# Forget bias from three bf16 pieces in one product, and a reordered passage into the sparse pairs, in a two-layer decoder trunk

## The chip, the cores and the metric

The kernel runs on one core of a Trainium2 chip. The metric is the device time of one execution in microseconds (us); lower is better. The engines are called PE (TensorE, matmuls), DVE (VectorE), ACT (ScalarE), POOL (GpSimd) and SP (SyncE, which issues the weight loads).

## What is computed

Two decoder layers over 256 tokens of width 2048, all in float32, one sequence. Layer 0 mixes with native sparse attention (8 heads: compressed, selected and window branches, gated) and multi-head latent attention (8 heads) behind one input projection. Layer 1 mixes with forgetting attention (FoX, 16 heads of 128). Each mixer is followed by a SwiGLU network; shifts, scales and gates come from a condition vector through `ada_w`. What the change touches, cut from the reference:

```python
# layer 0: compressed keys and values from blocks of 32 tokens, stride 16, plus a position term
blk = k[:, idx] + pos_emb[:, None, :]
return jax.nn.silu(blk @ w1) @ w2
# layer 1: forget bias of head h: cumulative log forget gates
cum = lax.cumsum(jax.nn.log_sigmoid((f + f_b).astype(jnp.float32)), axis=1).transpose(0, 2, 1)
logit = (jnp.einsum('bqhd,bkhd->bhqk', qq, k) * scale + cq[..., None] - cum[:, :, None, :])
p = masked_softmax(logit, kpos[None, :] <= t[:, None])
```

The residual is `x + g1 * y` with `g1` a row of 2048 gates, made from `ada_w` (accumulated in ACC, summed over partitions by PE) and a bias row in GROW.

## The kernel before

Every weight matrix is streamed in units of 1 MB through a ring of four slots (RAW). ACT rounds a unit to its high part (WHI, line 662), DVE subtracts for the low part (WLO, line 1858), and PE multiplies three times: high by high, low by high, high by low (lines 1129 to 1131). WHI and WLO hold two units each, taken in turn by the unit's number. Between the weight units stand "ada" units: DVE adds a 128-row slab of `ada_w`, times the condition, into ACC (line 1871). SP issues the loads in one fixed order; each waits until its slot of the ring is released, by a low part, an ada step or, for the compression weights, by PE.

The order of work on each engine is written out by hand, with semaphores between the engines; nothing is scheduled by a planner.

**The passage into the sparse pairs.** The input projection is eight chunks; chunk 5 and 6 are the latents of the second branch, chunk 7 (88 columns, line 1147) the gates and the rotary key. On PE follow: turning chunk 6 (L1195), the scores of pair 0 (L1431), the gate row's sum over partitions in four quarters (`finish((0, G1))`, L1176; quarters 2 and 3 reuse the banks of 0 and 1 and wait until DVE has read them), the turn of the gate tile (L1471), and then the loop over 8 pairs of heads. In iteration p stand a unit of the compression product (`cmp_unit`, L1411: 16 products of 30 stationary columns), scores p+1, values p-1 (L1460 to L1463) and the turn of pair p's probabilities (L1442). Pairs 0 to 3 are the selected branch, 4 to 7 the window branch. DVE does in this stretch: RMS scaling of chunk 6 (ST, L2104), its gain (TF, L2125), the low part CQL (L1965), the copy of the gate tile (GK, L2099), logits of pair 0 (L2159 to L2164), the four additions into GROW (L1882), gates (L2196, L2197), the blocks BF (L2206, eight additions), then per iteration logits, an ada step, outputs of the pair before. ACT does in each iteration the exponentials (L838) and the copy of the turned probabilities PT (L848); in iteration 7 the high part of the first MLA weight stands between the two.

BF lies in the room of AHI/ALO, the split input of the projection, so the blocks can be written only after the last projection product. GK shares the buffer TF with the latents, so it waits for CQL.

**FoX scores.** Eight pairs of heads (12 to 19), one batch (`fox_scores`) within each of eight chunks of the projection, after the chunk's first unit. For each head and each block of 128 queries a batch has three products into one bank: query by key (L1740), the bias (L1741: stationary a column of the identity broadcast to 128 columns over 16 rows, moving CUMT, the 16 heads' cumulative sums by token, f32), and the mask (L1742, bf16). CUMT is made once, during the chunk before: cumulative sums (CUM, L2605), turned on PE (L1777), scaled by DVE (L2608).

Of the kernel before, what the change touches and what calls it, by code (L numbers as in the profile page):

```python
# [23 lines left out]
KT = D // P  # L24
# [17 lines left out]
C_ID, C_UT, C_ONE, C_NEG, C_THR, C_INV, C_CM, C_CN = 0, 128, 256, 384, 512, 513, 545, 575  # L42
C_BLK, C_LEAD = 605, 609
C_ALL = 610

# [145 lines left out]
class Machine:  # L191

    def __init__(self, nc, t, ctx, known):
# [19 lines left out]
        self.WHI = sb("WHI", [P, 2, 2048], F32R)  # L213
        self.WLO = sb("WLO", [P, 2, 2048], F32R)

        ((self.AHI, self.ALO), (_, self.XG), (self.O, self.KN, self.RP, self.KRO, self.HCT, self.KCT, self.VCN), (_, self.BF)) = overlay(
            [("AHI", [P, KT, T], F32R), ("ALO", [P, KT, T], F32R)],
            [("XG_ROOM", [P, KT, T], F32), ("XG", [P, KT, T], F32)],
            [("O", [P, 16, T], F32), ("KN", [P, 8, T], F32), ("RP", [P, 2, 8, 64], F32), ("KRO", [P, 2, P], F32),
             ("HCT", [P, 2, 2, 30], F32), ("KCT", [P, 32], F32), ("VCN", [P, 2, P], F32)],  # L220
            [("O_ROOM", [P, 16, T], F32), ("BF", [P, 2, 32, 30], F32)])

# [21 lines left out]
        self.IDB = sb("IDB", [P, P], BF16)  # L244
        self.NEGB = sb("NEGB", [P, P], BF16)
        self.VC = sb("VC", [P, V_ALL])
        self.COND = sb("COND", [P, KT])
# [9 lines left out]
            [("KRR", [P, 2, 64], F32), ("COS", [P, 2, 32], F32), ("SIN", [P, 2, 32], F32)],  # L257
            [("Z", [P, 4, 2, 16], F32), ("CUM", [P, 2, 16], F32)])
        self.PF = sb("PF", [P, 2])
# [13 lines left out]
        self.PART = self.RS[:, 2, 4:6]  # L273
        self.CUMT, self.FZ, self.FE, self.FL = (self.TF[0:16, i, :] for i in range(4))
        self.GK = self.TF[0:88, 0, :]
        self.RB, self.RBS, self.GB, self.FB = (self.VC[:, a:b] for a, b in ((V_RB, V_RBS), (V_RBS, V_GB), (V_GB, V_FB), (V_FB, V_ALL)))
# [834 lines left out]
def tensor_program(block, nc, t, out, m):  # L1111

    @block.tensor
    def _(pe):
# [50 lines left out]

        def finish(v, blocks=range(KT)):

            pe.wait_ge(m["ada_used"].sem, ADA_DONE[v])
            acc = m.adder(v)
            if v[1] in (G1, G2):  # L1170
                if v == (1, G1):
                    wait("t_read", ("fox", m.fox_at["k", 3]))
                for q in range(4):
# [293 lines left out]
        scores(0)  # L1467
        finish((0, G1))
        wait("gk_kept", ("even_in", 7))
        for tb in range(2):  # L1470
            ins = turn(m.PS[:, 4, P * tb:P * tb + 88], m.GK[:, P * tb:P * tb + P], m.CON[0:88, C_ID:C_ID + 88])  # L1471
        m["gk_turned"].tick(ins, 0)
        wait("cmp_b", 0)
        for p in range(8):
            if p == 4:
                wait("cmp_b", 1)
            cmp_unit(p)
            if p == 0:
                wait("gates_in", ("even_in", 7))
                wait("row_read", ((0, G1), 3))  # L1480
            if p < 7:
                scores(p + 1)
            if p:
                values(p - 1)
            turn_p(p)
        values(7)
# [243 lines left out]
        def fox_scores(p):  # L1730
# [4 lines left out]
            for j in range(2):  # L1735
                h = m.pairs[p][1] + j
                bank = m.PS[:, 4 + j, :]
                for tb in range(2):
                    qs, n, at = slice(P * tb, P * tb + P), P + P * tb, P * tb
                    mm(bank[:, at:at + n], m.QT_F[:, h, qs], m.KT_F[:, h, 0:n], start=True, stop=False)  # L1740
                    mm(bank[:, at:at + n], m.CON[0:16, C_ID + h:C_ID + h + 1].to_broadcast([16, P]), m.CUMT[:, 0:n], start=False, stop=False)  # L1741
                    ins = mm(bank[:, at + n - P:at + n], m.IDB[:], m.NEGB[:], start=False, stop=True)  # L1742
# [30 lines left out]
        def cumulate_turned():  # L1773

            wait("cum_ready", 0)
            for tb in range(2):
                ins = turn(m.PS[0:16, 5, P * tb:P * tb + P], m.CUM[:, tb, :], m.ID)  # L1777
            m["cumt_done"].tick(ins, 0)
# [53 lines left out]
def vector_program(block, nc, t, out, m):  # L1832

    @block.vector
    def _(dve):
# [36 lines left out]

        def finish(v):

            layer, seg = v
            n = 2 * layer + (seg >= SH2)
            if seg in (G1, G2):
                wait("grow_bias", 2 * layer + (seg == G2))
                for q in range(4):
                    wait("ada_sum", (v, q))  # L1880
# [214 lines left out]
        def even_first(c):  # L2095
            if c.i == 7:
                chunk_done(c)
                dve.wait_ge(m["lo_split"].sem, m["lo_split"].value)
                m["gk_kept"].tick(V.tensor_copy(m.GK, m.acc(c.buf)[0:88, 0, 0:T]), c.key)  # L2099
# [6 lines left out]
        def bias_masked():  # L2106
            dve.wait_ge(m["bias_kept"].sem, m["bias_kept"].value)
            after = m.CON[:, C_NEG:C_NEG + P].unsqueeze(1).to_broadcast([P, 8, P])
            for at in (0, T):
                ins = TT(m.BIAS[:, :, at:at + P], m.BIAS[:, :, at:at + P], after, ALU.add)  # L2110
            link(ins)

        def even_second(c):
# [8 lines left out]
            else:  # L2122
# [3 lines left out]
                dve.wait_ge(m["tf_ready"].sem, m["tf_ready"].value)  # L2126
                split_lo(c.key, m.CQL[:, at:at + 4, :], m.TF[:], m.CQH[:, at:at + 4, :])

        def even_between(c, j):
# [4 lines left out]
            if c.i == 4 and j == 2:  # L2134
                angles()
        run(m.even_in[3:], even_first, even_second, between=even_between)


        def logits(p):
# [13 lines left out]
            elif name == "fox":  # L2153
                for j in range(2):
                    for tb in range(2):
                        cols = slice(P, 3 * P) if tb else slice(0, P)
                        ins = TS(dst[:, j, cols], m.PS[:, 4 + j, cols], FOX_SCALE, m.CUM[:, tb, h0 + j:h0 + j + 1], ALU.mult, ALU.add)
            else:
# [7 lines left out]
        def outputs(p):  # L2166
# [19 lines left out]
            else:  # L2186
# [11 lines left out]
        for i in range(2):  # L2198
            at = (V_PK, V_PV)[i]
            for g in range(2):  # L2200

                for half in range(2):
                    l0 = 16 * half
                    src = m.XT[:, 8 + 2 * i + g, l0:l0 + 240].rearrange("p (n l) -> p l n", l=16)
                    pos = m.VC[:, at + l0:at + l0 + 16].unsqueeze(2).to_broadcast([P, 16, 15])
                    ins = TT(m.BF[:, i, l0:l0 + 16, 15 * g:15 * g + 15], src, pos, ALU.add)  # L2206
                    m["cmp_b"].tick(ins, i)
        for p in range(8):
# [381 lines left out]
        def fox_between(c, j):  # L2590
# [11 lines left out]
            if c is fox_chunks[0] and j == 3:  # L2602
                fox_second(m.fox_in[1])
                wait("cum_done", 0)
                m["cum_ready"].tick(V.tensor_copy(m.CUM[:], m.PS[:, 4, 0:32].rearrange("p (b h) -> p b h", b=2)), 0)  # L2605
# [70 lines left out]
```

## Time and profile before

| | us |
|---|---|
| median of 3 runs | 2571.3 (2568.48 to 2573.88) |
| the profiled execution | 2571.42 |
| its span, first to last instruction | 2569.6 |
| PE busy | 2480.1 (97%) |
| DVE busy | 1708.0 (66%) |
| ACT busy | 1028.9 (40%) |
| mean granted TensorE clock | 0.985 |

Busy time is the union of an engine's instructions. A matmul's end is modelled, and matmuls overlap; how long one really keeps the engine is best read from the start of the next. The clock is a share of full speed, 1.00 being 2.4 GHz and 0.50 being 1.2 GHz.

### The profile page before, as it was taken

The numbers are of one execution on the slowest core, as the hardware profiler recorded it, in microseconds if no ns is written. First come the engines' busy times: TensorE is split into PE (matmuls) and PEld (weight loads), VectorE is DVE, ScalarE is ACT, GpSimd is POOL, SyncE is SP. The second block draws the span as 40 slices with busy tenths as digits, with TensorE's granted clock in tenths as the row PEclk, the third lists the DMA queues.
The fourth block names the chain that finished last, engine by engine and source line by source line (L and its number), as shares of the span: only waits on it lengthen the run. The fifth ranks groups of instructions, "written<-read, shape, count | busy, mean of one in ns | idle before, by whom it ended". The sixth has DMA issues, their size and how long they took to land.

```text
span 2569.6 us, 29279 instructions
## 1 busy us (share of the span) xinstructions
PE 2480.1 (97%) x11756; PEld 2011.1 (78%) x11756; DVE 1708.0 (66%) x1355; ACT 1028.9 (40%) x975; POOL 3.0 (0%) x9
## 2 busy tenths in 40 slices
PE   5899899999999999999999999999999999999998
PEld 3677577778878888888877888778788788888887
DVE  6878686886676767766766666668766554445446
ACT  2234344454333333343544444444543333333434
POOL 0000000000000000000000000000000000000000
PEclk8899999999999999999999999999999999999999
DMA  9989575868786877778788896889687655555553
GB/s 356 351 292 344 206 277 215 299 242 289 277 311 220 311 269 290 269 265 307 228 182 228 182 211 184 231 264 331 220 288 278 235 190 187 195 181 196 188 189 130
DMA packets 266196, 636.57 MB, mean 248 GB/s; under 512 B 15984, under 2 KB 26992, under 8 KB 244720
## 3 DMA queue, kind: packets, MB, share of 16 engines
q1 hardware_dynamic: 264800, 627.35, 73.7%
q0 software_dynamic: 720, 5.24, 0.6%
q10 hardware_dynamic: 576, 2.57, 0.2%
q8 instruction: 71, 1.16, 0.2%
q14 instruction: 29, 0.24, 0.0%
HBM read 633.03 MB, written 2.10 MB: 247 GB/s over the span
## 4 chain that ended last, share of the span: by engine, by line
PE 82%; DVE 8%; DMA 5%; ACT 3%; issue 2%; SPq 0%; DVEq 0%; ACTq 0%
PE PS L1129 23%; PE PS L1131 23%; PE PS L1130 23%; DVE WLO L1858 2%; ACT WHI L662 2%; DMA RAW<-in_fox_w_in 2%; DMA RAW<-in_even_w_in 1%; PE PS L1411 1%; DVE ACC L1871 1%; DMA PRO<-in_ada_w 1%; DVE ACC L1980 1%; PE PS L1431 1%; PE PS L1180 1%; PE PS L1697 1%; PE PS L1195 1%
## 5 line engine op out<-in xcount | busy, mean ns | idle before, releaser
L1129 PE MATMUL PS<-WHI,AHI 128*128 128x512 f32 x2024 | 796.3, 393 | 11.5 <-DVE WLO L1858 9.8
L1131 PE MATMUL PS<-WHI,ALO 128*128 128x512 f32 x2024 | 788.9, 390 | 0.0
L1130 PE MATMUL PS<-WLO,AHI 128*128 128x512 f32 x2024 | 788.4, 390 | 0.0
L1858 DVE TENSOR_TENSOR WLO<-RAW,WHI 128x2048 fp32r<-128x2048 f32 (+2 forms) x217 | 492.2, 2268 | 350.5 <-ACT WHI L662 350.2
L662 ACT ACTIVATE WHI<-RAW 128x2048 fp32r<-128x2048 f32 (+2 forms) x217 | 412.0, 1899 | 717.6 <-PE PS L1131 509.8
L2448 DVE TENSOR_TENSOR WLO<-RAW,WHI 128x2048 fp32r<-128x2048 f32 x174 | 398.8, 2292 | 351.6 <-ACT WHI L972 351.6
L972 ACT ACTIVATE WHI<-RAW 128x2048 fp32r<-128x2048 f32 x174 | 333.7, 1918 | 578.1 <-PE PS L1131 555.4
L1129 PEld LDWEIGHTS PS<-WHI,AHI 128*128 128x128 f32 x2024 | 380.4, 188 | 94.5 <-issue 7.1
L1131 PEld LDWEIGHTS PS<-WHI,ALO 128*128 128x128 f32 x2024 | 380.3, 188 | 80.3
L1130 PEld LDWEIGHTS PS<-WLO,AHI 128*128 128x128 f32 x2024 | 380.6, 188 | 76.7 <-issue 0.2
L1129 PE MATMUL PS<-WHI,GHI 128*128 128x512 f32 x864 | 340.9, 395 | 3.4 <-DVE WLO L1858 3.1
L1131 PE MATMUL PS<-WHI,GLO 128*128 128x512 f32 x864 | 337.0, 390 | 0.0
L1130 PE MATMUL PS<-WLO,GHI 128*128 128x512 f32 x864 | 336.7, 390 | 0.0
L1871 DVE SCALAR_TENSOR_TENSOR ACC<-RAW,COND,ACC 128x2048 f32<-128x2048 f32 x94 | 220.4, 2345 | 0.7
L1129 PEld LDWEIGHTS PS<-WHI,GHI 128*128 128x128 f32 x864 | 162.6, 188 | 40.2 <-issue 5.3
L1131 PEld LDWEIGHTS PS<-WHI,GLO 128*128 128x128 f32 x864 | 162.4, 188 | 34.2
L1130 PEld LDWEIGHTS PS<-WLO,GHI 128*128 128x128 f32 x864 | 162.7, 188 | 33.3 <-issue 0.5
L2459 DVE SCALAR_TENSOR_TENSOR ACC<-RAW,COND,ACC 128x2048 f32<-128x2048 f32 x60 | 140.7, 2345 | 0.1
L838 ACT ACTIVATE L<-L,NM 128x128 f32<-128x128 f32 x80 | 35.4, 446 | 62.4 <-DVE NM L2164 62.4
L1980 DVE SCALAR_TENSOR_TENSOR ACC<-PRO,COND,ACC 128x512 f32<-128x512 f32 x60 | 45.0, 750 | 6.9 <-DMA PRO<-in_ada_w 5.2
L1286 PE MATMUL PS<-WHI,AHI 128*128 128x512 f32 x96 | 41.5, 432 | 7.0 <-DVE ALO L1965 6.8
L2339 DVE TENSOR_TENSOR TF<-PS,GROW 128x1024 f32<-128x1024 f32 x28 | 34.2, 1221 | 14.7 <-PE PS L1131 14.7
(326 smaller groups left out, 1785.7 us busy)
## 6 DMA issues: line engine op xcount, KB each, us to landing
RAW<-in_ffn_w SPq DMA_DIRECT2D x264, 1024.0 KB, 5.2
RAW<-in_ada_w SPq DMA_DIRECT2D x176, 1024.0 KB, 5.9
RAW<-in_fox_w_in SPq DMA_DIRECT2D x64, 1024.0 KB, 8.2
RAW<-in_even_w_in SPq DMA_DIRECT2D x28, 1024.0 KB, 7.5
PRO<-in_ada_w SPq DMA_DIRECT2D x16, 1024.0 KB, 12.5
RAW<-in_even_w_out SPq DMA_DIRECT2D x16, 1024.0 KB, 7.3
RAW<-in_fox_w_out SPq DMA_DIRECT2D x16, 1024.0 KB, 6.7
GROW<-in_ada_b POOLq DMA_DIRECT2D x4, 1024.0 KB, 6.7
```

Source lines behind the costliest of these rows:

```text
L662: A(m.w_view(m.WHI, u), m.w_view(m.RAW, u), ACT.Copy).then_inc(m["hi_ready"].sem, 1)
L838: m["exp_done"].tick(A(m.L[:, b, h, cols], m.L[:, b, h, cols], ACT.Exp, bias=m.NM[:, b, j:j + 1], accum_out=m.SM[:, b, j:j + 1]), p)
L972: A(m.WHI[:, (up.w0 + j) % 2, :], m.RAW[:, (up.s0 + s) % RING, :], ACT.Copy).then_inc(m["hi_ready"].sem, 1)
L1129: mm(dst(tb), xh, whi[:, k, :], start=first and k == 0, stop=False)
L1130: mm(dst(tb), xh, wlo[:, k, :], start=False, stop=False)
L1131: ins = mm(dst(tb), xl, whi[:, k, :], start=False, stop=last and k == nk - 1)
L1286: mm(dst, xh, whi[:, k, :], start=kt == 0, stop=False)
L1858: TT(m.w_view(m.WLO, u), m.w_view(m.RAW, u), m.w_view(m.WHI, u).bitcast(F32), ALU.subtract).then_inc(m["lo_ready"].sem, 1)
L1871: STT(out=acc[:], in0=raw, scalar=m.COND[:, kt:kt + 1], in1=acc[:], op0=ALU.mult, op1=ALU.add).then_inc(m["ada_used"].sem, 1)
L1980: ins = STT(out=acc, in0=src, scalar=by, in1=acc, op0=ALU.mult, op1=ALU.add)
L2448: TT(m.WLO[:, (up.w0 + j) % 2, :], m.RAW[:, (up.s0 + s) % RING, :], m.WHI[:, (up.w0 + j) % 2, :].bitcast(F32), ALU.subtract).then_inc(m["l ...
L2459: STT(out=m.ACC[:], in0=m.RAW[:, slot, :], scalar=m.COND[:, col], in1=m.ACC[:], op0=ALU.mult, op1=ALU.add).then_inc(m["ada_used"].sem, 1)
```

## The change

Two things, independent of each other.

**Bias.** The cumulative sums are copied six times side by side (96 columns), so that turning them gives 96 rows. DVE scales them and makes three bf16 pieces: the rounded value in rows 0 to 31, the rounded rest in rows 32 to 63, the rounded rest of that in rows 64 to 95. A stationary matrix HEADB (bf16, a one in rows h, 32+h and 64+h of column h) picks head h and adds the three pieces in one bf16 product of 96 rows.

**Passage.** BF moves into half 1 of the WLO ring, the gate tile copy GK into PT. On DVE the blocks and the gate copy come before the gain of chunk 6, two of the four gate-row additions before the first logits, CQL behind them, the other two additions after the gates. On PE compression unit 0 comes between quarters 0, 1 and quarters 2, 3 of the gate row, and in the loop unit p+1 stands ahead of the turn of pair p (before: unit p ahead of scores p+1). DVE waits for the last compression unit before it writes the first MLA low part, since that takes BF's place.

```diff
+        (self.WLO,), (_, self.BF) = overlay(
+            [("WLO", [P, 2, 2048], F32R)],
+            [("BF_ROOM", [P, 2048], F32), ("BF", [P, 2, 32, 30], F32)])
...
-            [("O_ROOM", [P, 16, T], F32), ("BF", [P, 2, 32, 30], F32)])
-            [("Z", [P, 4, 2, 16], F32), ("CUM", [P, 2, 16], F32)])
+            [("Z", [P, 4, 2, 16], F32), ("CUM", [P, 2, 6, 16], F32)])
+        self.CUMB = self.TF[0:96, 0, 0:128].bitcast(BF16)
+        self.CUMV, self.CUMR = self.TF[0:96, 2, :], self.TF[0:96, 3, :]
-        self.GK = self.TF[0:88, 0, :]
+        self.GK = self.PT[0:88, 1, 0, 0:T]
 # tensor engine, passage
         scores(0)
-        finish((0, G1))
+        finish((0, G1), quarters=(0, 1))
         wait("gk_kept", ("even_in", 7))
+        wait("tf_ready", ("even_in", 6))
...
         wait("cmp_b", 0)
+        cmp_unit(0)
+        finish((0, G1), quarters=(2, 3))
+        wait("gates_in", ("even_in", 7))
         for p in range(8):
-            if p == 4:
-                wait("cmp_b", 1)
-            cmp_unit(p)
-            if p == 0:
-                wait("gates_in", ("even_in", 7))
-                wait("row_read", ((0, G1), 3))
             if p < 7:
                 scores(p + 1)
             if p:
                 values(p - 1)
+            if p == 3:
+                wait("cmp_b", 1)
+            if p < 7:
+                cmp_unit(p + 1)
+            if p == 0:
+                wait("row_read", ((0, G1), 3))
             turn_p(p)
 # tensor engine, FoX scores
-                    mm(bank[:, at:at + n], m.CON[0:16, C_ID + h:C_ID + h + 1].to_broadcast([16, P]), m.CUMT[:, 0:n], start=False, stop=False)
+                    mm(bank[:, at:at + n], m.HEADB[0:96, h:h + 1].to_broadcast([96, P]), m.CUMB[:, 0:n], start=False, stop=False)
 # vector engine, passage
         def even_between(c, j):
+            if c.i == 7:
+                blocks()
+                even_first(c)
...
+        finish((0, G1), (0, 1))
         logits(0)
-        finish((0, G1))
+        latent_low(m.even_in[6])
         wait("gk_turned", 0)
...
+        finish((0, G1), (2, 3))
         for p in range(8):
...
+        dve.wait_ge(m["row_used"].sem, m.cmp_in[1][-1].n + 1)
         lo(mla[0])
 # vector engine, FoX
-                m["cumt_ready"].tick(TS(m.CUMT, m.PS[0:16, 5, 0:256], -1.0 / FOX_SCALE, None, ALU.mult), 0)
+                link(TS(m.CUMV, m.PS[0:96, 5, 0:256], -1.0 / FOX_SCALE, None, ALU.mult))
+                link(V.tensor_copy(m.CUMB, m.CUMV))
+                link(TT(m.CUMR, m.CUMV, m.CUMB, ALU.subtract))
+                V.tensor_copy(m.CUMB[32:64], m.CUMR[32:64])
+                link(V.tensor_copy(m.CUMB[64:96], m.CUMR[64:96]))
+                link(TT(m.CUMR[64:96], m.CUMR[64:96], m.CUMB[64:96], ALU.subtract))
+                m["cumt_ready"].tick(V.tensor_copy(m.CUMB[64:96], m.CUMR[64:96]), 0)
```

`blocks()` holds the eight additions that stood ahead of the loop, and `latent_low` the subtraction that makes CQL.

## Rows read from the trace of the kernel before

**Rows 1.** The page, part 1: engine, busy us, share of the span, instructions.

```profile
PE 2480.1 (97%) x11756; PEld 2011.1 (78%) x11756; DVE 1708.0 (66%) x1355; ACT 1028.9 (40%) x975; POOL 3.0 (0%) x9
```

**Rows 2.** Timeline, PE, passage: start us, busy us, line, out<-in, count, idle before.

```profile
266.44 1.88 PE L1176 MATMUL PS<-ACC,CON 128*128 128x512 f32 x4
273.05 3.78 PE L1176 MATMUL PS<-ACC,CON 128*128 128x512 f32 x4 [4.73 <-DVE GROW L1882]
276.62 0.50 PE L1471 MATMUL PS<-CON,TF 88*128 88x88 f32 x2
279.90 5.33 PE L1411 MATMUL PS<-RAW,BF 128*30 128x256 f32 x16 [2.78 <-DVE BF L2206]
285.15 1.58 PE L1431 MATMUL PS<-XT 128*128 128x128 f32 x8
...
287.32 3.64 PE L1411 MATMUL PS<-RAW,BF 128*30 128x256 f32 x16
```

**Rows 3.** Windows: stretch, length, busy of PE, PEld, DVE, ACT, POOL, PEclk, DMA.

```profile
280.00:286.00 6.00, 6.00 (x21) 2.84 (x22) 2.92 (x5) 1.45 (x7) 0.00 (x0) 0.72 0.00 0
286.00:300.00 14.00, 14.00 (x83) 9.52 (x82) 10.36 (x18) 5.35 (x18) 0.00 (x0) 1.00 0.89 308
```

**Rows 4.** Timeline, DVE, the same passage.

```profile
265.33 1.66 DVE L2125 TENSOR_SCALAR TF<-PS,VC 128x256 f32<-128x256 f32 x4 [3.97 <-PE PS L1195]
268.53 1.23 DVE L1965 TENSOR_TENSOR CQL<-TF,CQH 128x1024 fp32r<-128x1024 f32 x1 [1.54 <-ACT CQH L673]
...
270.20 0.94 DVE L2159 SCALAR_TENSOR_TENSOR L<-PS,BIAS 128x768 f32<-128x768 f32 x1
...
272.30 1.29 DVE L1882 TENSOR_TENSOR GROW<-PS,GROW 128x512 f32<-128x512 f32 x2
...
277.91 3.81 DVE L2206 TENSOR_TENSOR BF<-XT,VC 128x240 f32<-128x240 f32 x8
```

**Rows 5.** Windows, a stretch of the FoX stage.

```profile
1400.00:1500.00 100.00, 100.00 (x478) 80.40 (x477) 63.28 (x71) 46.58 (x55) 0.00 (x0) 1.00 0.88 200
```

**Rows 6.** Timeline, all engines, end of the pair loop.

```profile
329.84 0.81 ACT L848 ACTIVATE PT<-PS 128x768 f32<-128x768 f32 x1 [2.50 <-PE PS L1442]
...
332.53 0.40 ACT L838 ACTIVATE L<-L,NM 128x128 f32<-128x128 f32 x1 [1.88 <-DVE NM L2164]
...
334.30 1.47 ACT L662 ACTIVATE WHI<-RAW 128x1536 fp32r<-128x1536 f32 x1
...
335.68 0.78 ACT L848 ACTIVATE PT<-PS 128x768 f32<-128x768 f32 x1
...
336.51 0.49 PE L1460 MATMUL PS<-NV,PT 128*128 128x128 f32 x2 [0.95 <-ACT PT L848]
```

**Rows 7.** Timeline, PE, first FoX score batch; the other seven repeat it.

```profile
1382.77 0.38 PE L1740 MATMUL PS<-KT_F,QT_F 128*128 128x128 f32 x2
1383.08 0.48 PE L1741 MATMUL PS<-TF,CON 16*128 16x128 f32 x2
1383.49 0.23 PE L1742 MATMUL PS<-NEGB,IDB 128*128 128x128 bf16 x1
1383.56 0.65 PE L1740 MATMUL PS<-KT_F,QT_F 128*128 128x256 f32 x2
1384.14 0.69 PE L1741 MATMUL PS<-TF,CON 16*128 16x256 f32 x2
1384.77 0.23 PE L1742 MATMUL PS<-NEGB,IDB 128*128 128x128 bf16 x1
...
1386.93 0.48 PE L1129 MATMUL PS<-WHI,AHI 128*128 128x512 f32 x1
```

**Rows 8.** Timeline, PE, bf16 products of the position bias.

```profile
96.28 1.36 PE L1320 MATMUL PS<-GROW,S 128*128 128x32 bf16 x48
```

**Rows 9.** Timeline, PE, one product pair of the MLA scores.

```profile
407.02 0.70 PE L1433 MATMUL PS<-QRK 64*128 64x256 f32 x2
```

**Rows 10.** Timeline, DVE, the scaling that makes CUMT.

```profile
1377.38 0.41 DVE L2608 TENSOR_SCALAR TF<-PS 16x256 f32<-16x256 f32 x1 [0.32 <-PE PS L1777]
```

More of the change, by code:

```diff
@@ L42 @@
 C_ID, C_UT, C_ONE, C_NEG, C_THR, C_INV, C_CM, C_CN = 0, 128, 256, 384, 512, 513, 545, 575
-C_BLK, C_LEAD = 605, 609
-C_ALL = 610
+C_BLK, C_LEAD, C_STACK = 605, 609, 610
+C_ALL = 642
 V_C, V_MIX, V_FFN, V_QN, V_KVN, V_FQ, V_FK, V_PK = 0, 16, 48, 80, 84, 88, 89, 90
@@ L67, in constants @@
     c[:, C_LEAD] = i % 32 == 0
+    c[:, C_STACK:C_STACK + 32] = i[:, None] % 32 == np.arange(32)[None, :]
     return c
@@ L213, in __init__ @@
         self.WHI = sb("WHI", [P, 2, 2048], F32R)
-        self.WLO = sb("WLO", [P, 2, 2048], F32R)
-        ((self.AHI, self.ALO), (_, self.XG), (self.O, self.KN, self.RP, self.KRO, self.HCT, self.KCT, self.VCN), (_, self.BF)) = overlay(
+        (self.WLO,), (_, self.BF) = overlay(
+            [("WLO", [P, 2, 2048], F32R)],
+            [("BF_ROOM", [P, 2048], F32), ("BF", [P, 2, 32, 30], F32)])
+        ((self.AHI, self.ALO), (_, self.XG), (self.O, self.KN, self.RP, self.KRO, self.HCT, self.KCT, self.VCN)) = overlay(
             [("AHI", [P, KT, T], F32R), ("ALO", [P, KT, T], F32R)],
@@ L219, in __init__ @@
             [("O", [P, 16, T], F32), ("KN", [P, 8, T], F32), ("RP", [P, 2, 8, 64], F32), ("KRO", [P, 2, P], F32),
-             ("HCT", [P, 2, 2, 30], F32), ("KCT", [P, 32], F32), ("VCN", [P, 2, P], F32)],
-            [("O_ROOM", [P, 16, T], F32), ("BF", [P, 2, 32, 30], F32)])
+             ("HCT", [P, 2, 2, 30], F32), ("KCT", [P, 32], F32), ("VCN", [P, 2, P], F32)])
         (self.GHI, self.GLO), (self.PRO,), (self.XT, self.CQH, self.CQL), (_, self.QN), (self.KT_F, self.V_F) = overlay(
@@ L245, in __init__ @@
         self.NEGB = sb("NEGB", [P, P], BF16)
+        self.HEADB = sb("HEADB", [P, 16], BF16)
         self.VC = sb("VC", [P, V_ALL])
@@ L273, in __init__ @@
         self.PART = self.RS[:, 2, 4:6]
-        self.CUMT, self.FZ, self.FE, self.FL = (self.TF[0:16, i, :] for i in range(4))
-        self.GK = self.TF[0:88, 0, :]
+        self.FZ, self.FE, self.FL = (self.TF[0:16, i, :] for i in range(1, 4))
+        self.CUMB = self.TF[0:96, 0, 0:128].bitcast(BF16)
+        self.CUMV, self.CUMR = self.TF[0:96, 2, :], self.TF[0:96, 3, :]
+        self.GK = self.PT[0:88, 1, 0, 0:T]
         self.RB, self.RBS, self.GB, self.FB = (self.VC[:, a:b] for a, b in ((V_RB, V_RBS), (V_RBS, V_GB), (V_GB, V_FB), (V_FB, V_ALL)))
@@ L1164, in unit, with finish @@
             ins.then_inc(m["w_used"].sem, 1)
-        def finish(v, blocks=range(KT)):
+        def finish(v, blocks=range(KT), quarters=range(4)):
             pe.wait_ge(m["ada_used"].sem, ADA_DONE[v])
@@ L1172, in finish @@
                     wait("t_read", ("fox", m.fox_at["k", 3]))
-                for q in range(4):
+                for q in quarters:
                     if q >= 2:
@@ L1776, in cumulate_turned @@
             for tb in range(2):
-                ins = turn(m.PS[0:16, 5, P * tb:P * tb + P], m.CUM[:, tb, :], m.ID)
+                ins = turn(m.PS[0:96, 5, P * tb:P * tb + P], m.CUM[:, tb].rearrange("p r h -> p (r h)"), m.ID)
             m["cumt_done"].tick(ins, 0)
@@ L1871, in ada, with finish @@
                 STT(out=acc[:], in0=raw, scalar=m.COND[:, kt:kt + 1], in1=acc[:], op0=ALU.mult, op1=ALU.add).then_inc(m["ada_used"].sem, 1)
-        def finish(v):
+        def finish(v, quarters=range(4)):
             layer, seg = v
@@ L1878, in finish @@
                 wait("grow_bias", 2 * layer + (seg == G2))
-                for q in range(4):
+                for q in quarters:
                     wait("ada_sum", (v, q))
@@ L1993, in _ @@
         V.tensor_copy(m.IDB[:], m.ID)
+        V.tensor_copy(m.HEADB[:], m.CON[:, C_STACK:C_STACK + 16])
         link(V.tensor_copy(m.NEGB[:], m.CON[:, C_NEG:C_NEG + P]))
@@ L2097, in even_first @@
                 chunk_done(c)
-                dve.wait_ge(m["lo_split"].sem, m["lo_split"].value)
                 m["gk_kept"].tick(V.tensor_copy(m.GK, m.acc(c.buf)[0:88, 0, 0:T]), c.key)
@@ L2111, in bias_masked, with blocks, latent_low @@
             link(ins)
+        def blocks():
+            for i in range(2):
+                at = (V_PK, V_PV)[i]
+                for g in range(2):
+                    for half in range(2):
+                        l0 = 16 * half
+                        src = m.XT[:, 8 + 2 * i + g, l0:l0 + 240].rearrange("p (n l) -> p l n", l=16)
+                        pos = m.VC[:, at + l0:at + l0 + 16].unsqueeze(2).to_broadcast([P, 16, 15])
+                        ins = TT(m.BF[:, i, l0:l0 + 16, 15 * g:15 * g + 15], src, pos, ALU.add)
+                        m["cmp_b"].tick(ins, i)
+        def latent_low(c):
+            at = 4 * (c.i - 5)
+            split_lo(c.key, m.CQL[:, at:at + 4, :], m.TF[:], m.CQH[:, at:at + 4, :])
         def even_second(c):
@@ L2126, in even_second @@
                 dve.wait_ge(m["tf_ready"].sem, m["tf_ready"].value)
-                split_lo(c.key, m.CQL[:, at:at + 4, :], m.TF[:], m.CQH[:, at:at + 4, :])
+                if c.i == 5:
+                    latent_low(c)
         def even_between(c, j):
@@ L2135, in even_between @@
                 angles()
-        run(m.even_in[3:], even_first, even_second, between=even_between)
+            if c.i == 7:
+                blocks()
+                even_first(c)
+        run(m.even_in[3:], even_first, even_second, between=even_between, last=lambda c: None)
         def logits(p):
@@ L2156, in logits @@
                         cols = slice(P, 3 * P) if tb else slice(0, P)
-                        ins = TS(dst[:, j, cols], m.PS[:, 4 + j, cols], FOX_SCALE, m.CUM[:, tb, h0 + j:h0 + j + 1], ALU.mult, ALU.add)
+                        ins = TS(dst[:, j, cols], m.PS[:, 4 + j, cols], FOX_SCALE, m.CUM[:, tb, 0, h0 + j:h0 + j + 1], ALU.mult, ALU.add)
             else:
@@ L2197, in _ @@
         m["gates_in"].tick(TT(m.GATES[:], gk[:, :, 0:24], m.GB[:].unsqueeze(1).to_broadcast([P, 2, 24]), ALU.add), ("even_in", 7))
[L2198 to L2207, printed above, removed]
+        finish((0, G1), (2, 3))
         for p in range(8):
@@ L2604, in fox_between @@
                 wait("cum_done", 0)
-                m["cum_ready"].tick(V.tensor_copy(m.CUM[:], m.PS[:, 4, 0:32].rearrange("p (b h) -> p b h", b=2)), 0)
+                m["cum_ready"].tick(V.tensor_copy(m.CUM[:], m.PS[:, 4, 0:32].rearrange("p (b h) -> p b h", b=2).unsqueeze(2).to_broadcast([P, 2, 6, 16])), 0)
             if c is fox_chunks[1] and j == 0:
                 wait("cumt_done", 0)
-                m["cumt_ready"].tick(TS(m.CUMT, m.PS[0:16, 5, 0:256], -1.0 / FOX_SCALE, None, ALU.mult), 0)
+                link(TS(m.CUMV, m.PS[0:96, 5, 0:256], -1.0 / FOX_SCALE, None, ALU.mult))
[5 more added lines that the diff above has]
+                m["cumt_ready"].tick(V.tensor_copy(m.CUMB[64:96], m.CUMR[64:96]), 0)
             if j == 2 and c.key in m.pair_in:
```

## The prediction

> **What bounds the kernel now.** I read the page's engine table first: TensorE (PE) is busy 2480.1 of 2569.6 us, 97% [rows 1]. So time can only be won where PE idles, where it runs at its lower clock, or by giving it less to do. The change touches two such places.
>
> The first is the passage from the input projection into the sparse pairs. The reader is to see four things in [rows 2]. After the first two quarter products of the gate row (L1176, 266.44 + 1.88 = 268.32) PE waits 4.73 us for VectorE (DVE), which has to add them into GROW. The other two quarters last 3.78 us although the first two took 1.88. Then PE waits 2.78 us for the blocks BF. The first compression unit (L1411) takes 5.33 us, the second 3.64. The granted clock explains the last: 0.72 over 280 to 286 us, 1.00 from 286 [rows 3]; the first unit ran mostly at 1.2 GHz behind the idle time, the second at 2.4. Why DVE is late stands in [rows 4]: latent scaling (TF) to 267.0, its low part to 269.8, first logits from 270.20, only then the two additions (272.30), and the blocks last of all (277.91).
>
> The second place is the forget-bias product in the FoX scores. Over 1400 to 1500 us PE is busy 100.00 of 100.00 us at clock 1.00 [rows 5], so there every matmul taken away counts in full, if nothing else becomes late.
>
> **Part 1, the passage.** DVE's new order puts the blocks and the copy of the gate/rotary-key tile ahead of the latent scaling. BF now lies in half 1 of WLO, whose last unit (odd, of the chunk before) is already consumed, so the blocks can start when DVE has scaled ST, at about 261.35 (an estimate from the trace: it is the end of the work before the 3.97 us idle in [rows 4]: 265.33 - 3.97 = 261.36). They take 3.81 us: 265.2. The copy takes 0.4: 265.6. TF takes 1.66: 267.25, against 266.99 now. All this fills idle DVE time and is ahead of PE.
>
> PE, from 268.32: it no longer waits. The turn of the gate tile takes 0.50 [rows 2] and needs the copy and TF (267.25): 268.8. Compression unit 0 at the full clock 3.6: 272.4. Meanwhile DVE makes additions 0 and 1 as their products end (1.29 for two in [rows 4], so 269.1), then the first logits (272.30 - 270.20 = 2.10: 271.2), the low part (1.23: 272.4), gates (0.5: 272.9). Quarters 2 and 3 on PE: 1.9, 274.3; their additions 275.0, behind PE's scores 1. Scores 1 and turn 0 together 287.32 - 285.15 = 2.17, unit 1 another 3.6: PE has both units and turn 0 done at 280.0. Now it has them done at 287.32 + 3.6 = 290.9. Gain 10.9 us. As a check by another sum: idle 4.73 + 2.78, quarters 3.78 - 1.88 = 1.90, clock 5.33 - 3.64 = 1.69; together 11.1.
>
> What is late next: in the loop each unit now stands ahead of the turn of its pair instead of behind it. For seven iterations that costs nothing, because turn p+1 comes a whole iteration later. At the end it does. Today ScalarE (ACT) empties turn 6 at 329.84, starts the last exponentials at 332.53 and has them done at 334.30, then splits the first MLA weight (1.47), copies PT at 335.68, and PE starts the last values at 336.51 after waiting 0.95 [rows 6]. All this shifts by 10.9, but turn 6 moves another 3.6 later (unit 7 is ahead of it). So ACT copies PT of pair 6 at 322.5 to 323.3, and the exponentials of pair 7, queued behind that copy on ACT, start at 323.3 instead of 332.53 - 10.9 = 321.6. The whole tail behind them (exponentials 1.77, split 1.4, copy 0.8) is 1.7 to 1.8 late: last values at 327.4 instead of 325.6. Part 1 nets **336.5 - 327.4 = 9.1 us**.
>
> The added wait of DVE ahead of the first MLA low part is for unit 7 of the compression, done at 321.7 in this schedule; DVE reaches it at about 326. Behind it are the outputs of pair 7 and all MLA low parts, so it would matter, but it is met 4 us before. SP's queue: loads are released by compression units and ada steps, both earlier, and no load is put past another. The prologue's DVE copy (HEADB) and 32 more constant columns I cost at nothing: the prologue waits for weights. Bounds: not above 10.9 (tail hidden); not below 5.7 (9.1 less 1.7 if the clock does not hold in unit 0, less 1.7 for a second late wait of the size of the tail's).
>
> **Part 2, the bias product.** Each of 8 score batches has two heads with one 128- and one 256-column bias product, f32, two passes. By the starts in [rows 7]: 1383.49 - 1383.08 = 0.41 and 1384.77 - 1384.14 = 0.63, so 2 x (0.41 + 0.63) = 2.08 us of a batch of 1386.93 - 1382.77 = 4.16. New: one bf16 pass with 96 rows. No row has that shape. Nearest: the mask product, bf16, 128 columns, 1383.56 - 1383.49 = 0.07; and 48 bf16 products of 32 columns in 1.36 us, 0.028 each with their weight loads [rows 8]. From 32 to 128 columns that is 0.042/96 a column, so 256 columns come to 0.13. New sum 2 x (0.07 + 0.13) = 0.40; saved 1.68 a batch, times 8 = **13.4 us**. Lower bound: half the old price, one pass for two, saves 1.04 a batch, 8.3. Upper bound: the QK products beside it get cheaper too, down to those of the sparse scores, where four such take at most 1.58 (285.15, [rows 2]); then the batch is 1.58 + 0.40 + 4 x 0.07 = 2.26, saves 1.90, 15.2 in all.
>
> Why the 16-row product is so dear: a 64-row one in the MLA scores is busy 0.70 us for its two passes of 256 columns [rows 9], the 16-row one 0.69 [rows 7], so the price is not the rows but standing between 128-row products. The Trainium skill (TensorE: Matmul & The Clock Gate, Part 2) says that a weight load is pulled ahead of running matmuls when the row groups don't conflict or it goes to the background buffer, and that its time goes by columns, not rows. By the second half alone 96 rows are free; by the first, a 96-row tile among 128-row ones could stay unhidden as the 16-row one does. That is the first rival.
>
> DVE pays for the split: instead of one 0.41 us scaling at 1377.38 [rows 10] seven linked steps on at most 96 x 256, six more of 0.2 to 0.4, some 2.3 us: ready at about 1380, while the scores that wait for it start at 1382.77 [rows 7]. Behind it on DVE is the low part of the next unit, needed after the scores: 1382.2 against 1385.2. Hidden; uncovered it would cost those 2.3 once. Copying CUM sixfold and turning 96 instead of 16 columns are some 0.1 us each. The freed 1.7 us do not make low parts late: DVE is busy 63.28 of 100 [rows 5].
>
> **Sum.** 9.1 + 13.4 = 22.5. The profiled execution took 2571.42 us (span 2569.6), practically the median 2571.3. So 2571.4 - 22.5 = **2549 us**.
>
> **Rivals.**
> A, the weight loads of 96-row products stay unhidden. For: 16- and 64-row products both show it. Against: bf16 loads are short, 0.028 us with their matmul [rows 8]. Price: near the lower bound, 8.3 instead of 13.4: 2571.4 - 17.4 = 2554.
> B, the passage gives more back: ACT's queue (PT copy, exponentials, split) ends the pair loop, and a second such wait follows in the MLA stage. Part 1 at 5.7: 2552. For: PE does wait there now. Against: every load and low part of that stage hangs on events that shift by the same 9.
> C, the neighbours shrink too and the tail is hidden: 10.9 + 15.2: 2545.
> D, the change does not do what it says: PE leaves the quarters but waits for TF or the gate copy. It would need DVE to be 4 us later than reckoned, and ends near 2553.
> E, slower: the low clock, which now ends by itself at 286, persists through the pair loop, since the thin units, turns and row sums come before PE has had a long dense stretch. An iteration costs (336.51 - 279.90) / 8 = 7.1 [rows 2, 6]; by 5.33 against 3.64 about half more at the low clock, 3.5 each. The seventh such iteration takes the last of the 22.5 us gained; all eight cost 28 and give 2577. The Trainium skill's same page (on transposes) says that they don't count as busy the same way for the clock. Against: with just this mix the clock came back at 286 and stayed [rows 3].
>
> **Chances.** Forecast (2546 to 2552) 0.62; A 0.15; B 0.10; C 0.06; D 0.03; E 0.04. The range, 2544 to 2556, takes in both ends of both parts but for E and the corner where all goes badly. No change that can be told is 0.2%, 5.1 us: 2566 to 2576. Faster 0.95, same 0.02, slower 0.03, E's gentler half being the middle case.
>
> **What would show it.** Right: no PE wait for GROW or BF between 268 and 280, granted clock 1.00 there, all L1411 units near 3.6; scores 2 starting near 280; last values near 327.4 after a wait of 0.6 or more behind ACT; score batches of 2.5 us instead of 4.16, with the bias products at 0.07 and 0.13; 1400 to 1500 still 100% busy. Wrong: a 96-row product above 0.2 us, PE waiting for WLO inside the FoX stage, a new wait of DVE on the last compression unit, or a shift of the MLA stage by less than 8 us.

## The result, and the profile after

| | before | after |
|---|---|---|
| median, us | 2569.9 (4 runs, 2567.2 to 2573.9) | 2541.3 (4 runs, 2538.8 to 2543.3) |
| profiled execution, us (span) | 2571.4 (2569.6) | 2538.8 (2536.8) |
| PE busy, us | 2480.1 | 2459.8 |

The ratio is 0.9887, 95% interval 0.987 to 0.9904: 28.6 us or 1.1% faster. 2549 was forecast, 2544 to 2556 the range: the direction was right, and the time lies 7.7 us below the forecast and below the range. The gain itself was put 6.1 us too low (22.5 against 28.6); the other 1.5 us are the starting point, a profiled execution of 2571.4 where the median is 2569.9.

The page of the changed kernel, its span and its engine table (busy us, share, instructions):

```profile
span 2536.8 us, 29223 instructions
...
PE 2459.8 (97%) x11724; PEld 2007.0 (79%) x11724; DVE 1709.1 (67%) x1362; ACT 1027.2 (40%) x975; POOL 3.0 (0%) x9
```

PE's share is again 97% [rows 1]; between the two profiled executions 20.3 us of its work are gone and 12.5 us of its idle time.

The passage on PE, timeline (start, busy us, line, output and inputs, count); it answers to [rows 2]:

```profile
264.67 1.88 PE L1181 MATMUL PS<-ACC,CON 128*128 128x512 f32 x4
266.38 0.32 PE L1477 MATMUL PS<-CON,PT 88*128 88x88 f32 x2
266.63 3.64 PE L1416 MATMUL PS<-RAW,BF 128*30 128x256 f32 x16
270.20 1.98 PE L1181 MATMUL PS<-ACC,CON 128*128 128x512 f32 x4
...
273.42 3.64 PE L1416 MATMUL PS<-RAW,BF 128*30 128x256 f32 x16
...
277.70 1.48 PE L1436 MATMUL PS<-XT 128*128 128x128 f32 x8
```

There is no idle time in it. Quarters 2 and 3 take 1.98 where they took 3.78, unit 0 takes 3.64 where it took 5.33, and scores 2 start at 277.70, 13.03 us behind the first quarter. Before they started at 290.89, 24.45 us behind it, as PE's timeline of the kernel before shows:

```profile
286.57 0.82 PE L1442 MATMUL PS<-CON,L 128*128 128x128 f32 x6
...
290.89 1.58 PE L1431 MATMUL PS<-XT 128*128 128x128 f32 x8
```

DVE in the same stretch, against [rows 4]:

```profile
259.70 3.93 DVE L2131 TENSOR_TENSOR BF<-XT,VC 128x240 f32<-128x240 f32 x8
...
265.82 1.45 DVE L1891 TENSOR_TENSOR GROW<-PS,GROW 128x512 f32<-128x512 f32 x2 [0.29 <-PE PS L1181]
```

The blocks stand at 259.70 in time that DVE spent waiting before, and the first two additions at 265.82, while PE still makes their products. The granted clock (the column behind POOL's busy time) is full over 265 to 280. Before it was 0.50 over quarters 2 and 3 and 0.72 over 280 to 286 [rows 3]; the first line is the kernel before, the second the changed one:

```profile
273.00:277.00 4.00, 3.95 (x6) 1.62 (x6) 1.42 (x3) 0.00 (x0) 0.00 (x0) 0.50 0.00 0
...
265.00:280.00 15.00, 15.00 (x73) 8.75 (x72) 12.73 (x21) 7.83 (x20) 0.00 (x0) 1.00 0.55 167
```

The end of the pair loop, all engines, against [rows 6]:

```profile
320.05 0.81 ACT L853 ACTIVATE PT<-PS 128x768 f32<-128x768 f32 x1 [4.47 <-PE PS L1447]
...
320.92 0.49 PE L1465 MATMUL PS<-NV,PT 128*128 128x128 f32 x2 [0.90 <-ACT PT L853]
...
322.51 1.47 ACT L667 ACTIVATE WHI<-RAW 128x1536 fp32r<-128x1536 f32 x1
...
323.89 0.79 ACT L853 ACTIVATE PT<-PS 128x768 f32<-128x768 f32 x1
...
324.73 0.49 PE L1465 MATMUL PS<-NV,PT 128*128 128x128 f32 x2 [1.19 <-ACT PT L853]
```

Here PE waits for ACT twice, 0.90 for the copy of pair 6 and 1.19 for the copy of pair 7, where it waited once before, 0.95 [rows 6]. That is the price of the new loop order.

The first FoX score batch, against [rows 7]:

```profile
1371.41 0.38 PE L1749 MATMUL PS<-KT_F,QT_F 128*128 128x128 f32 x2
1371.63 0.22 PE L1750 MATMUL PS<-TF,HEADB 96*128 96x128 bf16 x1
1371.69 0.22 PE L1751 MATMUL PS<-NEGB,IDB 128*128 128x128 bf16 x1
1371.75 0.65 PE L1749 MATMUL PS<-KT_F,QT_F 128*128 128x256 f32 x2
1372.23 0.27 PE L1750 MATMUL PS<-TF,HEADB 96*128 96x256 bf16 x1
1372.35 0.22 PE L1751 MATMUL PS<-NEGB,IDB 128*128 128x128 bf16 x1
...
1373.43 0.48 PE L1134 MATMUL PS<-WHI,AHI 128*128 128x512 f32 x1
```

A batch takes 1373.43 - 1371.41 = 2.02 us where it took 4.16 (2.01 and 4.16 without the rounding of the two starts). The bias products take 0.06 and 0.12. But the QK products (query by key) in front of them are cheaper too: 0.22 for 128 columns (0.31 before) and 0.48 for 256 (0.58 before). Of the 2.15 us that a batch loses, 1.74 are the bias products, 0.38 the QK products and 0.03 the masks.

### The profile page after: what moved, and what is told of

The parts are those of the page before. It is cut to its first block, busy times and chain, and to the rows that moved or that the text cites. A ratio compares the mean times of both kernels' runs of the same rounds, so it can differ in the third digit from the quotient of the medians.

```text
span 2536.8 us, 29223 instructions
## 1 busy us (share of the span) xinstructions
PE 2459.8 (97%) x11724; PEld 2007.0 (79%) x11724; DVE 1709.1 (67%) x1362; ACT 1027.2 (40%) x975; POOL 3.0 (0%) x9
## 4 chain that ended last, share of the span: by engine, by line
PE 85%; DVE 7%; DMA 3%; issue 2%; ACT 2%; SPq 0%; DVEq 0%; ACTq 0%
PE PS L1134 24%; PE PS L1136 24%; PE PS L1135 24%; DVE WLO L1867 2%; ACT WHI L667 1%; DVE ACC L1880 1%; PE PS L1416 1%; DMA RAW<-in_fox_w_in 1%; DMA PRO<-in_ada_w 1%; DVE ACC L1989 1%; PE PS L1436 1%; PE PS L1200 1%; PE PS L1185 1%; PE PS L1706 1%; DMA RAW<-in_ada_w 1%
```

## The experiments

Times are medians of the runs; each set of kernels ran on one chip, with the kernel before beside it (medians 2569.2 to 2570.2), and the ratio is to that one. "Passage" is the stretch from the first gate-row quarter to the last start of a values product (L1460 in the kernel before). Passage and score batch are read from one trace of each kernel; a batch of 2.01 and one of 2.02 differ only by rounding.

```
kernel           median us  ratio to before (95%)    passage us   score batch us
before           2569.9                              71.0         4.16
after            2541.3     0.9887 (0.987-0.9904)    60.9         2.02
e1_bias          2552.9     0.9935 (0.9921-0.9949)   71.7         2.02
e2_passage       2558.8     0.9964 (0.995-0.9978)    61.0         4.16
e3_after_again   2542.4     0.9893 (0.9877-0.9908)   60.9         2.02
e5_f32_96        2548.9     0.9924 (0.9907-0.9941)   60.9         2.99
e6_bf16_16       2543.5     one run                  60.9         2.83
e7_blocks_only   2546.4     0.9909 (0.9895-0.9922)   65.7         2.01
e8_sums_late     2546.5     0.9901 (0.9882-0.992)    60.9         2.01
e9_tail          2540.7     0.9893 (0.9876-0.9909)   59.4         2.01
e10_tail_hi      2540.7     0.9884 (0.987-0.9899)    59.4         2.01
e11_mla_rows     2537.3     0.9867 (0.985-0.9884)    60.9         2.02
e12_all          2538.7     0.9877 (0.986-0.9894)    59.4         2.02
```

**e1_bias**: the kernel before with only the bias hunks.

```diff
-  mm(bank[:, at:at + n], m.CON[0:16, C_ID + h:C_ID + h + 1].to_broadcast([16, P]), m.CUMT[:, 0:n], ...)
+  mm(bank[:, at:at + n], m.HEADB[0:96, h:h + 1].to_broadcast([96, P]), m.CUMB[:, 0:n], ...)
```

> Only the bias product changed, passage as before. Theory (two independent parts that add up; a 96-row product keeps its weight load hidden beside 128-row ones): a FoX score batch takes 2.1 us instead of 4.16, 8 batches 16.8 us, so 16 to 18 us below the kernel before. Rival (the bias is worth only my 13.4 and the rest of the surplus came from the waits around the FoX gates): 13 to 14. The trace shows whether PE still waits 2.7 us for WLO between the last two batches and the output product.

By the ratio 16.7 us (13.1 to 20.3), by the medians 17.3. The interval alone doesn't shut out the rival's 13 to 14; the trace does: all 8 batches take 2.01, so 8 x 2.15 = 17.2 us are gone there. The wait for WLO is still there, so the surplus did not come from it:

```profile
PE PS L1133 <- DVE WLO L1862: 3.1, 1, 3.1
```

(PE's waits between the last batch and the output product: us, times, longest.) The passage is 0.8 us longer than in the kernel before, and its granted clock differs too: 0.50 over 277 to 281, where the kernel before had 0.92 over 277 to 280.

**e2_passage**: the kernel before with only the passage hunks (BF in WLO, GK in PT, the orders of DVE and PE).

> Only the passage changed, bias product as before. Theory: 10 us gained up to the last values of the pair loop, one more in the MLA stage, 10 to 12 below the kernel before in all. Rival (the two parts need each other, or the rest of the 28.6 came from somewhere else): less than 9 or more than 13.

11.4 by the medians, 9.3 (5.7 to 12.9) by the ratio, which leaves the rival's "less than 9" open; the passage itself is 10.0 shorter in the trace, as in the changed kernel. The parts add up: 16.7 + 9.3 = 26.0, or 17.3 + 11.4 = 28.7, against 28.6.

**e3_after_again** and **e4_before_again**: the two kernels unchanged.

> The changed kernel once more, on the chip of the two partial ones. If the parts add up, its gain over the kernel before is that of e1 plus that of e2 within 2 us. Its trace shows how much of the 1.7 us of the prologue and of the 4.2 us after the last batch comes back by chance.

> The kernel before once more, for its trace. Theory: the wait of 2.7 us for WLO near 1702 us, with the low clock behind it, is a late weight load and differs from execution to execution; then it is absent or elsewhere here. Rival: it belongs to the kernel before, and stands again near 1702 us.

e3: 27.8 below the kernel before by the medians, as the parts sum. Its first quarter starts at 266.5, in the first profile of the same kernel at 264.7, before the change at 266.4: the 1.7 us that the prologue seemed to bring are scatter. e4, a single run, took 2575.7, and between its last batch and the output product PE again waited for WLO, 2.1 us in two waits; that speaks for the rival, and the section on the prediction takes it up.

**e5_f32_96** and **e6_bf16_16** take apart what the bias product's price is made of. e6 leaves out the two lower bf16 pieces, so it computes a coarser bias and is there for its timing only.

```diff
 e5, against the changed kernel
-  mm(..., m.HEADB[0:96, h:h + 1].to_broadcast([96, P]), m.CUMB[:, 0:n], ...)
+  mm(..., m.CON[0:96, C_ID + h:C_ID + h + 1].to_broadcast([96, P]), m.CUMV[:, 0:n], ...)
 e6, against the changed kernel
+  mm(..., m.HEADB[0:16, h:h + 1].to_broadcast([16, P]), m.CUMB[0:16, 0:n], ...)
```

> The changed kernel, but the bias product in f32 again, over 96 rows (a column of the identity, zero in the 80 added rows, times the f32 sums); two passes as before the change, rows as after it. Theory (what made the old product dear was its 16-row tile: weight loads beside 128-row products were not hidden, on either side): the 128- and 256-column products take about 0.22 and 0.48 us, as the QK products of the sparse scores do, a batch 1.4 + 1.4 + 0.3 = 3.1 us, 8 us slower than the changed kernel in all. Rival (f32 itself was dear, rows don't matter): 0.41 and 0.63 as before, a batch 4.16, 17 us slower.

> The changed kernel, but the bias product only over the first 16 rows, that is with the first bf16 piece alone (the two lower pieces are left out). Theory (the tile of 16 rows between 128-row ones exposes weight loads): more than the 0.06 and 0.12 us of the 96-row product, about 0.10 to 0.2 more for each, and the QK product behind the mask unchanged; a batch 2.5 to 2.9 us. Rival (one bf16 pass is cheap whatever its rows): a batch 2.1 us.

Timeline of PE in a batch of e5, f32 over 96 rows:

```profile
1370.71 0.38 PE L1749 MATMUL PS<-KT_F,QT_F 128*128 128x128 f32 x2
1370.93 0.39 PE L1750 MATMUL PS<-TF,CON 96*128 96x128 f32 x2
1371.15 0.22 PE L1751 MATMUL PS<-NEGB,IDB 128*128 128x128 bf16 x1
1371.21 0.65 PE L1749 MATMUL PS<-KT_F,QT_F 128*128 128x256 f32 x2
1371.70 0.60 PE L1750 MATMUL PS<-TF,CON 96*128 96x256 f32 x2
1372.13 0.22 PE L1751 MATMUL PS<-NEGB,IDB 128*128 128x128 bf16 x1
...
1373.70 0.48 PE L1134 MATMUL PS<-WHI,AHI 128*128 128x512 f32 x1
```

and of e6, bf16 over 16 rows:

```profile
1370.26 0.38 PE L1749 MATMUL PS<-KT_F,QT_F 128*128 128x128 f32 x2
1370.58 0.22 PE L1750 MATMUL PS<-TF,HEADB 16*128 16x128 bf16 x1
1370.73 0.23 PE L1751 MATMUL PS<-NEGB,IDB 128*128 128x128 bf16 x1
1370.80 0.65 PE L1749 MATMUL PS<-KT_F,QT_F 128*128 128x256 f32 x2
1371.38 0.28 PE L1750 MATMUL PS<-TF,HEADB 16*128 16x256 bf16 x1
1371.59 0.23 PE L1751 MATMUL PS<-NEGB,IDB 128*128 128x128 bf16 x1
...
1373.09 0.48 PE L1134 MATMUL PS<-WHI,AHI 128*128 128x512 f32 x1
```

In e5 the f32 product takes 0.22 and 0.43, not 0.41 and 0.63: the same two passes, the same columns, only more rows. In e6 the single bf16 pass takes 0.15 and 0.21, not 0.06 and 0.12, and the QK products are back at 0.32 and 0.58; I had expected them unchanged. Both rivals fall. The old batch of 4.16 loses 1.17 by the rows alone (2.99) and 1.34 by the type alone (2.83); both together take it to 2.01. A 16-row tile costs about 0.1 us on either side of it, whatever its type; the second f32 pass, which follows a 16-row pass, costs that 0.1 again (0.41 for two passes of 128 columns against 0.22). 96 rows cost nothing of that.

The rows of PEld (the engine's weight loads) show where the 0.1 us arises: the loads of the bias product's tile in the kernel before, and in e5:

```profile
1383.08 0.29 PEld L1741 LDWEIGHTS PS<-TF,CON 16*128 16x128 f32 x2
...
1370.82 0.30 PEld L1750 LDWEIGHTS PS<-TF,CON 96*128 96x128 f32 x2
```

Over 16 rows the load starts together with its own product (1383.08), 0.20 us behind the QK pass in front of it. Over 96 rows it starts with that QK pass, 0.11 us ahead of its own product (1370.93), so most of it runs while another product does. By the medians e5 is 7.6 us slower than the changed kernel, for 8 x 0.97 = 7.8.

**e7_blocks_only** and **e8_sums_late** take apart the passage.

```diff
 e7, PE: all quarters ahead of unit 0; DVE: all additions behind the low part
-        finish((0, G1), quarters=(0, 1))
+        finish((0, G1))
...
-        finish((0, G1), quarters=(2, 3))
 e8, DVE only
-        finish((0, G1), (0, 1))
         logits(0)
         latent_low(m.even_in[6])
+        finish((0, G1), (0, 1))
```

> The changed kernel with only the blocks (and the gate copy) early: all four quarters of the gate row ahead of compression unit 0 on PE, and all four additions behind the first logits and the low part on DVE. Theory: the wait for GROW returns at some 3 us (DVE reaches the additions at about 269 instead of 265.8), quarters 2 and 3 lose up to 1.8, and the low clock comes back for unit 0 if the idle time does it (1.7 more): 4 to 7 us slower than the changed kernel. Rival (the early blocks alone bring it, PE would catch up): within 2 us.

> The changed kernel with DVE's first two additions behind the first logits and the low part, PE's order unchanged. Theory (compression unit 0 between the quarters covers DVE by itself): the first addition ends near 270.0, when PE comes to quarter 2 (270.2), so nothing is lost, or at most 0.5 us. Rival (the split additions are what freed PE): PE waits for GROW 2 us or more.

PE in e7:

```profile
272.92 3.44 PE L1181 MATMUL PS<-ACC,CON 128*128 128x512 f32 x4 [3.01 <-DVE GROW L1890]
...
276.45 3.64 PE L1416 MATMUL PS<-RAW,BF 128*30 128x256 f32 x16
```

The wait for GROW is back at 3.01, quarters 2 and 3 take 3.44 instead of 1.98, and unit 0 keeps 3.64. The quarters lose what was expected; but the low clock fell on them alone and was over when unit 0 began (276.45), which was not:

```profile
272.00:277.00 5.00, 4.08 (x9) 1.88 (x10) 2.75 (x5) 0.00 (x0) 0.00 (x0) 0.66 0.00 0
277.00:282.00 5.00, 5.00 (x26) 2.69 (x25) 2.06 (x5) 3.39 (x10) 0.00 (x0) 1.00 0.14 25
```

The passage is 4.7 us longer than the changed kernel's, the median 4 to 5. So the early blocks and the early gate copy alone bring 5.3 of the 10.0 us, and unit 0 between the quarters the rest. In e8 the passage is 60.9 as in the changed kernel, and PE does not wait: halving the additions on DVE brings nothing as long as unit 0 covers them. Its median is higher than the changed kernel's, but its ratio's interval holds both.

**e9_tail** and **e10_tail_hi** mend the end of the loop.

```diff
 both, PE
-            if p < 7:
+            if p < 6:
                 cmp_unit(p + 1)
...
             turn_p(p)
+            if p == 6:
+                cmp_unit(7)
 e10, ACT
-            exps(p)
             if p == 7:
                 hi(m.mla_in[0].w[0])
+            exps(p)
             turned(p)
```

> The changed kernel with the turn of pair 6 ahead of the last compression unit again (only the last iteration). Theory (the new loop order costs its two waits behind ScalarE's copy at the loop's end, 0.90 + 1.19 us against 0.95 before): from the start of the gate row's products to the last values start 59.5 us instead of 60.9 to 325.6, about 1.4 us less, and the MLA stage keeps most of it. Rival (the MLA stage is paced by its loads and takes it back): nothing at its end.

> As e9_tail, and ScalarE splits the first MLA weight ahead of the last exponentials instead of behind them. Theory: the copy of pair 7 no longer queues behind 1.4 us of splitting, so the last values start another 0.3 to 0.5 us earlier than in e9. Rival (the weight lands later than 317 us, and the exponentials wait for it): as e9, or up to 1.5 us worse.

The end of the loop in e10:

```profile
316.63 0.81 ACT L853 ACTIVATE PT<-PS 128x768 f32<-128x768 f32 x1 [0.96 <-PE PS L1447]
...
317.33 1.48 ACT L667 ACTIVATE WHI<-RAW 128x1536 fp32r<-128x1536 f32 x1
...
322.38 0.81 ACT L853 ACTIVATE PT<-PS 128x768 f32<-128x768 f32 x1 [1.42 <-PE PS L1447]
...
323.25 0.49 PE L1465 MATMUL PS<-NV,PT 128*128 128x128 f32 x2 [0.90 <-ACT PT L853]
```

ACT copies pair 6 3.4 us earlier in e10 (316.63 against 320.05), and the passage is 1.6 us shorter (59.4), in e9 as in e10, for 1.4 expected; the further 0.3 to 0.5 of e10 did not come. Moving the split frees ACT (its last copy now waits 1.42 for PE to turn the probabilities of pair 7), so PE sets the end. Of the 1.6 us nothing can be told in the medians (2540.7 against 2541.3 and 2542.4), nor in the traces a stage later: from the first quarter to the first MLA scores it is 127.3 to 128.8 us in e9, e10 and e12, and 126.8 to 129.9 in the seven traces with a passage of 60.9 or 61.0. That fits the rival, but the scatter is larger than what was to be seen.

**e11_mla_rows** and **e12_all** carry the finding about rows to the MLA scores; e12 has e10's edits too. ScalarE writes the key's two halves into two tiles, DVE zeroes the rest of both once.

```diff
-                        rows = slice(64 * j, 64 * j + 64)
-                        extra = (m.QRK[rows, 1 + h // 2, qs], m.QRK[rows, 0, 0:n])
+                        extra = (m.QRK[:, 1 + h // 2, qs], m.QRK[:, 5 * j, 0:n])
...
+        V.memset(m.QRK[64:128, 0, :], 0.0)
+        link(V.memset(m.QRK[0:64, 5, :], 0.0))
```

> The changed kernel with the rotary product of the MLA scores over 128 rows instead of 64: the key stands in two tiles, each with zeros in the other head's half. Theory (a tile of fewer row groups between 128-row ones exposes weight loads, and this holds in the MLA scores too): f32 products of 128 and 256 columns fall from 0.41 and 0.63 to 0.22 and about 0.46, both kinds, so a batch of 8 products falls from 4.16 to 2.8 us; 4 batches, 5 us in all, if PE bounds that stage. Rival (other engines pace the stage; PE is 95 percent busy there): less than 2 us at the end of the stage.

> e10_tail_hi and e11_mla_rows together. If both theories hold 6 to 7 us below the changed kernel, about 2535 us, and 35 below the kernel before. If the loads pace the MLA stage, it is no better than the better of the two.

PE in the first MLA score batch of the changed kernel, and of e11:

```profile
393.33 0.49 PE L1438 MATMUL PS<-QRK 64*128 64x128 f32 x2
393.75 0.70 PE L1436 MATMUL PS<-KN,QN 128*128 128x256 f32 x2
394.38 0.70 PE L1438 MATMUL PS<-QRK 64*128 64x256 f32 x2
395.00 0.49 PE L1436 MATMUL PS<-KN,QN 128*128 128x128 f32 x2
```

```profile
395.87 0.39 PE L1442 MATMUL PS<-QRK 128*128 128x128 f32 x2
396.10 0.60 PE L1440 MATMUL PS<-KN,QN 128*128 128x256 f32 x2
396.53 0.59 PE L1442 MATMUL PS<-QRK 128*128 128x256 f32 x2
396.96 0.38 PE L1440 MATMUL PS<-KN,QN 128*128 128x128 f32 x2
```

The rotary products fall from 0.42 and 0.62 us to 0.23 and 0.43, and the batch (eight products, from 393.02 to 397.09 and from 395.65 to 398.27) from 4.07 to 2.62. The other three batches fall from 4.08 to 2.44, so the four make 6.4. Of these the stage keeps 4.3 (66.5 to 62.2 us from the first MLA score to the product behind the wait for DVE's output, and 62.2 again in e12): that wait grew from 1.2 to 2.2 us, and one of 0.8 is new. e11 is the fastest version, 2537.3, 4 to 5 us below the changed kernel by the medians; the intervals of the two ratios overlap. e12 is no better than e11 (2538.7 for about 2535 expected), so of the two mends the second is the one worth keeping.

## Why the prediction was wrong

**The bias product: the step that failed.** Forecast 13.4, measured 8 x 2.15 = 17.2. The term of 1.68 a batch held the bias product alone and left the QK products beside it at their old price; they fell too, by 0.38 a batch, and the bias products by 1.74. My upper bound of 15.2 let them shrink, but took them from the busy time 1.58 of four such products, whose end is modelled, instead of from the start of the next; by the starts they take 1.42 (286.57 - 285.15, the turn's start less their own), and the bound would have been 16.5, near what came. So even the two upper ends together, 10.9 + 15.2, stayed 2.5 us short of the gain.

The reason given was wrong as well. From equal busy times over 16 and 64 rows I concluded that the price is not the rows but standing between 128-row products. e5 keeps the place and the type, changes only the rows, 16 to 96, and the extra price is gone; e11 does the same from 64 to 128. Rows do decide, and equal times over 16 and 64 couldn't show it. The Trainium skill (TensorE: Matmul & The Clock Gate, Part 2) has a weight load pulled ahead when the row groups don't conflict or when it goes to the background buffer. The first condition alone does not sort these rows: behind a 128-row product the load of a 16- or 64-row tile starts only with its own product, one of 96 or 128 rows starts 0.11 us or more ahead of it. Its sentence that row count doesn't matter to a weight load's own time agrees (0.18 to 0.19 us in f32 over 16, 64, 96 and 128 rows); what the load costs between other products does depend on it. What puts 96 rows with 128 and not with 64 stays open.

**The passage: right, 0.9 us too small.** Forecast 9.1, measured 10.0 (70.96 to 60.95). The gain up to scores 2 was 24.45 - 13.03 = 11.4 for 10.9: I took the gate turn at 0.50, which it had only at the low clock (266.63 - 266.38 = 0.25 now), and the first two quarters at their busy time of 1.88, where the next product starts 1.71 later. The tail cost 1.4 to 1.6 for 1.7 to 1.8, by the mechanism named: ACT's exponentials queued behind a later copy. The added wait for the last compression unit shows nowhere. The clock gave back what the sum assumed.

**Rivals.** Half of C came, the shrinking neighbours, but not the hidden tail; it had a chance of 0.06 and 2545. A, B, D and E did not: no 96-row product above 0.12 us, no wait inside the FoX stage, the clock full from 265 to 300 with the thin units, turns and row sums that E named.

**The rest.** 10.0 + 17.2 = 27.2 of the 28.6 us between the medians, within what the medians scatter. The two first profiled executions lie 32.8 us of span apart, 5.6 more. 1.7 of it is the start of the passage, 264.7 for 266.4, and that went back to 266.5 in e3. 4.2 is the stretch from the last FoX values to the next layer's shift sum, 122.0 before and 117.8 after. There a weight lands late (in the kernel before ACT waits 5.69 us for it) and PE waits about 2 to 3 us. It did so in all four traces of kernels that lack one part or both (120.6 to 122.4), and in three of the other ten (119.8 to 121.9; the other seven 117.4 to 118.0). Whether the two parts together make that wait rarer, or this is luck, stays open. DVE's split of the sums cost what was reckoned: 2.6 us at 1366.1, done 2.7 us before the scores.

## What to carry to other kernels

Read the price of a matmul from the start of the next, and look at its neighbours: a product over 16 or 64 rows between full ones makes the one in front dearer too. Padding with zero rows can pay without any change of type: 1.17 us of a FoX batch in e5, and 4.3 us of the MLA stage in e11. In the FoX batch the type alone was worth a little more (1.34), and the two together most. When an engine idles because another is late, look for work that it can do in between. What that work needs must then come early (here the blocks, which unit 0 reads); other steps of the late engine needn't be reordered, as e8 shows of the additions. And a filler that is moved ahead of a step delays whatever hangs on that step: check the last iteration, where nothing covers it.

## What was not expected of the hardware

- Row tiles, by the start of the next product, between 128-row products and at full clock: f32, two passes, 128 and 256 columns: 0.41 and 0.63 us over 16 or 64 rows, 0.22 and 0.43 over 96 or 128. bf16, one pass: 0.15 and 0.21 over 16 rows, 0.06 and 0.12 over 96.
- Behind 3.01 us of idle time e7 shows a granted clock of 0.66 over 272 to 277 us, and 1.00 over the next 5. The kernel before, idle for 4.73 us and then for 2.78 more, shows 0.50 over 273 to 277, 0.92 over 277 to 280 and 0.72 over 280 to 286: the low level twice, over the quarters and over unit 0. e1, with the same work in the passage, stayed low in between.
- Over the fourteen traces the passage starts anywhere from 264.4 to 268.0 us, and 1.9 us apart in two traces of the same kernel (264.7 and 266.5). Part of it is PE's waits for low parts of the weights: in the latest, e7, it waits 1.8 us for one at 217 us, in the earliest, e6, for none there.
